# Head with x tiles 3 to 7 gated on half of v's weights, v's norms in batches, and pool weights times projection as one matrix formed on the chip

## The reference, cut to what matters

```python
h = rmsnorm(x, g_mix); proj = h @ w_in             # a | u,v | gate_a | gate_b
a = proj[..., :512]                                # pooling branch, 4 groups of 128 columns
z = gelu(proj[..., 512:1536])                      # u and v of the gating branch
gate_a, gate_b = sigmoid(proj[..., 1536:2560]), sigmoid(proj[..., 2560:])
# pooling: per group g, window w = 2, 4, 8, 16
p = window_sum(a_g, w) / min(w, pos+1) - a_g
pa = einsum('btgc,gcd->btgd', p, w_pool).reshape(B, T, 512) * s_pool
# gating: chunks of 128 rows, causal 128 x 128 matrix per group
v = rmsnorm(z[..., 512:], g_v)
sg = u * (tril(w_s) @ v + b_s)
merged = gate_a * (pa @ w_pool_out) + gate_b * (sg @ w_gmlp_out)
x = x + merged @ w_out
h2 = rmsnorm(x, g_ffn)
x = x + (silu(h2 @ w_gate) * (h2 @ w_up)) @ w_down  # d_ff 2816
y = rmsnorm(x, g_final)
```

## Time and profile before

| | us |
|---|---|
| median of 3 runs (lowest, highest) | 832.25 (831.86, 832.78) |
| profiled execution, its own time | 831.42 |
| span of its slowest core (core 2), first to last instruction | 829.6 |
| spans of the 8 cores | 826.4 to 829.6 |
| PE busy in the span | 805.8 (97%) |
| DVE, ACT, POOL busy | 380.8 (46%), 225.0 (27%), 96.2 (12%) |

### The profile page before, as it was taken

The page is one execution under the profiler, slowest core; times in us unless marked ns, Lnnn a source line. Parts: engine busy times, 40 slices in busy tenths (PEclk is TensorE's granted clock), DMA queues, the critical chain, the costliest instruction groups (busy, mean ns, idle before and its releaser), DMA issues.

```text
span 829.6 us, 12893 instructions; the slowest of 8 cores (826.4 to 829.6 us)
## 1 busy us (share of the span) xinstructions
PE 805.8 (97%) x4423; PEld 425.6 (51%) x4474; DVE 380.8 (46%) x618; ACT 225.0 (27%) x458; POOL 96.2 (12%) x154
## 2 busy tenths in 40 slices
PE   5999999999999999999999999999999999999996
PEld 3465666645666666644444444444444444444442
DVE  3776444468222222265776935446711111115357
ACT  2654322224211211120136352322321111110023
POOL 2720000012000000000312000011200000000001
PEclk9999999999999999999999999999999999999998
DMA  7894155684974543354977417688576444336313
GB/s 167 182 181 84 26 77 77 102 122 86 198 114 69 80 74 66 63 92 65 144 238 112 77 28 135 112 170 136 95 117 102 77 77 77 66 62 102 51 48 155
DMA packets 57315, 85.14 MB, mean 103 GB/s; under 512 B 23373, under 2 KB 23749, under 8 KB 57236
## 3 DMA queue, kind: packets, MB, share of 16 engines
q0 software_dynamic: 30352, 57.97, 45.3%
q1 hardware_dynamic: 26755, 26.09, 11.3%
q10 hardware_dynamic: 146, 0.27, 0.1%
HBM read 128.72 MB, written 9.01 MB: 166 GB/s over the span
## 4 chain that ended last, share of the span: by engine, by line
PE 84%; DVE 6%; issue 3%; DMA 2%; POOL 2%; ACT 2%; DVEq 0%; SPq 0%; POOLq 0%; ACTq 0%
PE ps L347 81%; DMA xbuf<-xp 2%; POOL rs L384 1%; DVE xbuf L367 1%; ACT junk L375 1%; ACT junk L992 1%; DVE xbuf L984 1%; PE ps L746 1%; PE ps L742 1%; DVE ybuf L1017 1%; DVE hb L404 0%; POOL rs L1003 0%; PE ps L695 0%; DVE shr L627 0%; DVE xbuf L874 0%
## 5 line engine op out<-in xcount | busy, mean ns | idle before, releaser
L347 PE MATMUL ps<-hT,ring 128*128 128x384 bf16 (+2 forms) x2698 | 484.1, 337 | 1.2
L347 PEld LDWEIGHTS ps<-hT,ring 128*128 128x128 bf16 x2720 | 265.5, 98 | 206.3
L347 PE MATMUL ps<-ring,ovl 128*128 128x512 bf16 x939 | 207.3, 379 | 1.1
L846 DVE TENSOR_TENSOR ovl<-ftmp,ps 128x384 bf16<-128x384 f32 (+2 forms) x110 | 64.2, 584 | 233.8 <-PE ps L347 226.5
L347 PEld LDWEIGHTS ps<-ring,ovl 128*128 128x128 bf16 x960 | 93.5, 98 | 113.8 <-issue 2.2
L844 ACT ACTIVATE ftmp<-ps 128x384 f32<-128x384 f32 (+2 forms) x110 | 56.3, 515 | 232.0 <-PE ps L347 232.0
L267 POOL DMA_DIRECT2D ring<-wpk x60 | 45.0, 750 | 493.8 <-PE ps L347 459.9
L944 DVE TENSOR_TENSOR xbuf<-xbuf,ps 128x512 f32<-128x512 f32 x64 | 43.4, 687 | 41.2 <-PE ps L347 41.1
L347 PE MATMUL ps<-ovl,ring 128*128 128x384 bf16 (+2 forms) x317 | 62.0, 337 | 0.2
L812 DVE TENSOR_TENSOR shr<-shr,ps 128x384 f32<-128x384 f32 (+2 forms) x40 | 23.4, 585 | 83.3 <-PE ps L347 74.5
L992 ACT ACTIVATE junk<-xbuf 128x512 bf16<-128x512 f32 (+1 forms) x34 | 21.3, 627 | 124.0 <-DVE xbuf L984 120.9
(11 more groups left out here) (90 smaller groups left out, 346.8 us busy)
## 6 DMA issues: line engine op xcount, KB each, us to landing
ring<-wpk POOLq DMA_DIRECT2D x48, 1024.0 KB, 11.2
xbuf<-xp SPq DMA_DIRECT2D x16, 512.0 KB, 6.6
yp<-ybuf SPq DMA_DIRECT2D x11, 512.0 KB, 3.4
ring<-wpk POOLq DMA_DIRECT2D x8, 512.0 KB, 13.0
ring<-wpk POOLq DMA_DIRECT2D x4, 768.0 KB, 8.1
yp<-shr SPq DMA_DIRECT2D x4, 512.0 KB, 2.6
AB<-xp SPq DMA_DIRECT2D x2, 512.0 KB, 6.9
shr<-xp SPq DMA_DIRECT2D x2, 512.0 KB, 11.6
```

What stands on the lines that cost most here:

```text
L347: ins = e.matmul(out=out, lhsT=lhs_fn(i), rhs=rhs_fn(i), start=(i == 0), stop=(i == n - 1))
L846: P.op('dve', lambda e: e.tensor_tensor(out=actT[:, f, c0:c0 + W], in0=ftmp[:, fi, :W], in1=PS[bU][:, :W], op=ALU.mult), reads=[('ftmp', f ...
```

## The change

- Loads: tiles 0, 1, 2 and the samples are issued at once. Ring block 0 is loaded in two halves (`ring_issue_halves`), both after tile 0 has landed; tiles 3 to 7 wait for the first half. Blocks 0 and 1 are read in pieces of 2048 and 4096 elements. Block 1 is issued at step 7, the constants at 8, block 2 at 9.
- v: a tile's eight matmuls may stand in two groups of four (`v_part`), and for the first tiles they do. gelu(v) goes to its own buffer per tile (`vg`, in the space of `mergedT`; samples in `ftmp`), the squares come some steps later, and POOL makes the means and rs of three tiles in one pair of operations (`v_rs`).
- The rows of g_v and two small vectors are copied on DVE at step 3 (`row_later`); the transpose of w_s moves from g = 0 to g = 2; the window sums of g = 2 are deferred too, but for their first three operations.
- `b4` is gone, and `paT`. ACT scales `w_pool`, which is handed over transposed, with `s_pool` (four operations of 128x128); for each q PE multiplies it with the quarter of `w_pool_out` (four matmuls of 256 columns), ACT copies the products to `mpo`, and the gates stage multiplies `mpo` with `pooled`. `mpo` is kept for `s` = 1, whose blocks hold `w_gmlp_out` alone. In the gates the product with `sgT` now stands ahead of the one with `pooled`.

```diff
-WPIECE = 1024
+WPIECE = [2048 if i < 1 else 4096 if i < 2 else 1024 for i in range(len(WBLOCKS))]
...
+        vg = ovl[:, 8 * TW + 9 * 512:8 * TW + 9 * 512 + 8 * 1024].bitcast(F32).rearrange("p (n c) -> p n c", n=8)
...
-        blocks = offs * NSUP
+        blocks = list(offs)
+        for (o_, e_), blk in zip(offs, WBLOCKS):
+            blocks.append((o_ + 128 * 1024, 1024) if blk[0][0] == 'w_po' else (o_, e_))
...
+        def ring_issue_halves(j, after=()):
+            slot = j % NSLOT
+            off, ne = blocks[j]
+            for h_ in range(2):
+                dst = ring[:, slot, h_ * (ne // 2):(h_ + 1) * (ne // 2)]
+                src = wpk[0:1, off + h_ * 64 * ne:off + (h_ + 1) * 64 * ne].rearrange("o (p e) -> (o p) e", p=128)
+                P.dma('pool',
+                      (lambda e, dst=dst, src=src: e.dma_start(out=dst, in_=src)),
+                      'wh%d' % h_, reads=list(after), writes=[('ring', slot, h_)])
             rstate['issued'] = j + 1
...
-        for slot in range(2, 8):
-            xload(0, slot, after=[('x', 1, 0)])
+        xload(0, 2)
         cdma('pool', ident_b[:, :], c_ident[:, :], 'ident_b', own='c_idb')
-        ring_issue(0)
+        ring_issue_halves(0, after=[('x', 0, 0)])
+        for slot in range(3, 8):
+            xload(0, slot, after=[('ring', 0, 0)])
...
-            ring_issue(1)
             cdma('pool', ws_nat[:, :, :], w_s.rearrange("g i j -> i g j"), 'ws_nat', own='c_wsnat')
-            cdma('pool', wpool_b[:, :, :], w_pool.rearrange("g c d -> c g d"), 'wpool', own='c_wpool')
             cdma('pool', bs_row[:, :], b_s[0:1, :], 'bs_row', own='c_bsrow')
...
+            cd(ybuf[:, 2, 0:512], w_pool[:, :], ('ybuf', 2))
...
+                    def fn(e, wv=wv):
+                        ins = None
+                        for i in range(4 * h_, 4 * h_ + 4):
+                            ins = e.matmul(out=PS[b][:R, :], lhsT=hT[:, i, col0:col0 + R], rhs=wv[:, i, :],
+                                           start=(i == 0), stop=(i == 7))
+                        return ins
+                    P.op('pe', fn, reads=[cres_[h_]] + hT_res([slot]), writes=[('ps', b)])
+
+                def v_mm(t_):
+                    if t_ == 0:
+                        v_part(0, 0)
+                    elif t_ == 1:
+                        v_part(1, 0)
+                        v_part(0, 1)
+                    elif t_ == 2:
+                        v_part(1, 1)
+                        v_part(2, 0)
+                        v_part(2, 1)
+                    else:
+                        v_part(t_, 0)
+                        v_part(t_, 1)
...
+                def v_rs(lo, hi):
+                    ka, kb = kv[lo], kv[hi - 1] + 1
+                    P.op('pool', lambda e: e.tensor_scalar(out=ms[:, ka:kb], in0=ss[:, ka:kb], scalar1=1.0 / 512,
+                                                           scalar2=EPS, op0=ALU.mult, op1=ALU.add),
+                         reads=[('ss', k_) for k_ in range(ka, kb)], writes=[('ms', k_) for k_ in range(ka, kb)])
+                    P.op('pool', lambda e: e.tensor_tensor(out=rs[:, ka:kb], in0=ms[:, ka:kb],
+                                                           in1=mhalf[:, 0:1].to_broadcast([128, kb - ka]), op=ALU.pow),
+                         reads=[('ms', k_) for k_ in range(ka, kb)] + ['mhalf'],
+                         writes=[('rs', k_) for k_ in range(ka, kb)])
...
+                vsq_at = {9: (0, 1), 10: (2, 3), 11: (4, 5), 12: (6,), 13: (7,), 14: (8,)}
+                vrs_at = {11: 0, 12: 3, 14: 6}
-                for i_ in range(n_ + 8):
-                    at(i_ - 3, do_v)
+                for i_ in range(n_ + 6):
+                    at(i_ - 4, v_mm)
...
+                    if i_ == 3:
+                        while row_later:
+                            row_later.pop(0)()
...
-                    at(i_ - 6, lambda t_: vst[t_][0]())
-                    at(i_ - 6, lambda t_: vst[t_][1]())
-                    if i_ == 5:
+                    at(i_ - 5, v_gelu)
+                    for t_ in vsq_at.get(i_, ()):
+                        v_sq(t_)
+                    if i_ == 7:
+                        ring_issue(1)
+                    if i_ == 8:
                         late_pool_consts()
                         mid_sp_consts()
-                    if i_ == 8:
+                    if i_ == 9:
                         ring_issue(2)
+                    if i_ in vrs_at:
+                        lo_ = vrs_at[i_]
+                        v_rs(lo_, lo_ + 3)
+                        for t_ in range(lo_, lo_ + 3):
+                            v_out(t_)
...
-                if s == 0 and g == 0:
+                if s == 0 and g == 2:
...
-                pool_chain(defer=(g == 3))
+                if g == 3:
+                    for _ in range(3):
+                        deferred_ops.pop(0)()
+                pool_chain(defer=(g >= 2))
...
-                    for (c0, W, tl) in nts:
-                        b = bank()
-                        pres = [('pooled', g)] + ([('pooled', g, 's')] if c0 + W > TPS else [])
-                        P.op('pe', lambda e, b=b, g=g, c0=c0, W=W: e.matmul(
-                            out=PS[b][:, :W], lhsT=wpool_b[:, g, :], rhs=pooled[:, g, c0:c0 + W],
-                            start=True, stop=True),
-                             reads=pres + ['wpool'], writes=[('ps', b)])
-                        P.op('act', lambda e, b=b, g=g, c0=c0, W=W: e.activation(
-                            out=paT[:, g, c0:c0 + W], in_=PS[b][:, :W], func=AF.Copy, scale=spT[:, g:g + 1]),
-                             reads=['spT'], writes=[('paT', g, c0), ('ps', b)])
...
-                if g < 3:
-                    b4_list[g]()
+            if s == 0:
+                for g_ in range(4):
+                    P.op('act', lambda e, g_=g_: e.activation(out=wpool_b[:, g_, :],
+                                                              in_=ybuf[:, 2, g_ * 128:(g_ + 1) * 128],
+                                                              func=AF.Copy, scale=spT[:, g_:g_ + 1]),
+                         reads=[('ybuf', 2), 'spT'], writes=[('wpool', g_)])
             while deferred_ops:
...
+                        if s == 0 and dl == 0 and c0 == 0:
+                            for h_ in range(2):
+                                bM = bank()
+
+                                def mpo_mm(e, bM=bM, h_=h_, pow_=pow_):
+                                    ins = None
+                                    for j_ in range(2):
+                                        ins = e.matmul(out=PS[bM][:, j_ * 256:(j_ + 1) * 256],
+                                                       lhsT=wpool_b[:, 2 * h_ + j_, :], rhs=pow_[:, 2 * h_ + j_, :],
+                                                       start=True, stop=True)
+                                    return ins
+                                P.op('pe', mpo_mm, reads=fres + [('wpool', 2 * h_), ('wpool', 2 * h_ + 1)],
+                                     writes=[('ps', bM)])
+                                P.op('act', lambda e, bM=bM, h_=h_, q=q: e.activation(
+                                    out=mpo[:, 2 * h_:2 * h_ + 2, q * 256:(q + 1) * 256],
+                                    in_=PS[bM][:, :].rearrange("p (j c) -> p j c", j=2), func=AF.Copy),
+                                     writes=[('mpo', q, h_), ('ps', bM)])
...
-                        P.op('pe', mm_group(PS[bP][:, :W],
-                                            lambda i, dl=dl, pow_=pow_: pow_[:, i, dl * 128:(dl + 1) * 128],
-                                            lambda i, c0=c0, W=W: paT[:, i, c0:c0 + W], 4),
-                             reads=fres + [('paT', gg, c0) for gg in range(4)], writes=[('ps', bP)])
...
+                        P.op('pe', mm_group(PS[bP][:, :W],
+                                            lambda i, d=d: mpo[:, i, d * 128:(d + 1) * 128],
+                                            lambda i, c0=c0, W=W: pooled[:, i, c0:c0 + W], 4),
+                             reads=[('mpo', q, h_) for h_ in range(2)] + [('pooled', gg) for gg in range(4)]
+                             + ([('pooled', gg, 's') for gg in range(4)] if c0 + W > TPS else []), writes=[('ps', bP)])
...
```

108 lines of the change are left out of this document (73 added, 35 removed).

## The result

The changed kernel took 835.17 us (833.76 to 836.52, 5 runs) against 832.25 (831.08 to 832.78, 5 runs) before: a ratio of 1.0043, 95% interval 1.0031 to 1.0054. By the ratio it is slower by some 3.6 us (by the medians alone 2.9), where 824.0 was forecast and 821 to 828.5 was the range. The times in this document are medians of all executions of a kernel, also of those in which the cores of a die ran at a lower granted clock; the ratios leave those out. The profiled execution took 835.17, its slowest core 833.6. Where before all cores lay within a few us, there are now two groups, of 824 to 827 and of 832 to 834.

A forecast was written before the change was run, and what follows sets the result against it. It took PE's own work and the start of stage 2 (a), which sets the end one for one, as the bound. From 831.4: -4.7 - 1.4 - 3.56 + 1.75 + 0.1 = -7.8, so 823.6, given as 824.0; range 821 to 828.5.

The forecast's parts named there:

- issue near 25, as before: Head, POOL's queue: ring block 1, behind the eighth norm, is issued near 25 and lands at 35, before stage a at 37.3.
- 15 us are enough: SP's constants: `w_pool`, the last, is not read before 52, and 15 us suffice for its landing.
- rival 3: Start of a: ring block 1, issued late, lands at 47.7 and a waits for it; 834.0 us, chance 0.05.
- Block 2 ... costs nothing: Ring block 2, for u: it has 14 us more than block 1, so its later issue costs 0.
- The clock behind a wait: Behind PE's wait in u: a lowered clock cost core 3 0.8 us; its removal is only in part 2's bound of -2.2.
- The head, -4.7: Stretch up to stage 2 (a): a's start on the slowest core moves from 42.0 to 37.3; bounds -7 and 0.
- The rate of 0.15 MB in one us: Head's loads: the ring's queue alone moves 0.15 MB per us, so half of v's weights (0.52 MB) costs 3.5 us.
- the first half would have the engines for itself: Head's loads: block 0's first half uses the engines from 8.3, lands near 12; the second shares with x 3 to 7.
- rival 1: Head: DMA engines are the bound, or PE stays at 1.2 GHz; a starts at 40, 826.3 us, chance 0.21.
- Part 2, -1.4: Waits in u: PE's 1.40 us wait for DVE's window sums goes; bounds 0 and -2.2.
- Part 3: `b4` removed: -3.56 us on PE; added 16 matmuls +1.75 and the gates' wait for `mpo` +0.1.
- The batch of v's norms: Head: 18 POOL operations become 6, off PE's path; window sums start 5.3 us behind a's start, not 8.7.

The follow-up runs named there:

- e2: Changed kernel with ring block 1 issued at step 5 of the head's loop, not step 7: 828.30 us, ratio 0.9967 to the kernel before.
- e9: e3 with ring block 1, the constants and ring block 2 at steps 7, 8, 9, not 5, 5, 8: 837.87 us, ratio 1.0076 to the kernel before.
- e1: Changed kernel with SP's constants waiting for x tile 7, not ring block 1: 836.52 us, ratio 1.0044 to the kernel before.
- e17: e6 with 20 more matmuls without a reader ahead of tile 3's transposes: 826.84 us, ratio 0.9944 to the kernel before.
- e5: Changed kernel with x tiles 3 to 7 waiting for x1, not the first half of block 0: 835.60 us, ratio 1.0042 to the kernel before.
- e16: e6 without loading block 0's second half (1 MB less), as many matmuls: 824.37 us, ratio 0.9909 to the kernel before.
- e3: Changed kernel with every hunk of the head taken back, the rest kept: 828.51 us, ratio 0.9955 to the kernel before.
- e6: Changed kernel with the edits of e5 and e2 together: 827.71 us, ratio 0.9962 to the kernel before.
- e13: e6 with ring block 1 in pieces of 1024 elements, not 4096: 828.61 us, ratio 0.9959 to the kernel before.
- e14: e6 with 48 more matmuls without a reader, 16 ahead of v and 32 behind tile 4's transposes: 830.38 us, ratio 0.9978 to the kernel before.
- e4: Changed kernel with SP's constants waiting for ring block 2, not block 1: 844.35 us, ratio 1.0147 to the kernel before.

## Why the prediction was wrong, step by step

- **"issue near 25, as before"** is the step that turned the sign: the cost of moving block 1 by two steps was put at nothing. I put ring block 1 behind the eighth norm and worked out 25 from gelu and squares that all came 3 to 4 us later. It was issued at 29.2 in the mean. Moved back by two steps it goes at 23.8 and the kernel is faster than before (e2); the old head loses as well when block 1 and what stands behind it move later by as much (e9).
- **"15 us are enough"** for SP's constants looked at `w_pool` alone. All of them, `sel` and `ident_f` with their readers in u ahead of `w_pool`'s, hang on block 1's landing; they took 16.5 and 18.7 on core 1. My rival 3 had the right place (block 1's landing) and the wrong victim: it asked only when a itself would wait for the ring, and gave 834.0 with a chance of 0.05. In the changed kernel no core waited for the ring ahead of a or in u; they waited for what was gated on it. And "Block 2 ... costs nothing" held only while the constants were the later ones (e1).
- **The clock behind a wait**, which I charged with 0.8 on one core as the earlier trace rows, cost 2.2 on core 1. The Trainium skill, TensorE: Matmul & The Clock Gate, "What's actually happening", says that the low clock is the default and sustained work lifts it. This trace agrees: granted 0.50 from 62 to 68 on core 1, while cores 0 and 4, which did not wait, have 1.00. That each such wait costs the clock is not so: e1's core 4 waited 2.90 in u and kept 1.00.
- **The head, -4.7**, did not come: a's latest start is 42.5 for 42.0, its mean 41.1 for 40.0, which two single profiles can't tell from no change. Of core 1's miss of 11.8 it is 3.7. Two terms, from the forecast's 36.7 to 41.1: tile 3's transposes at 23.8, not 20.5, and from there to a 17.3, not 16.2. The second is the clock: at full clock it is 15.4 (e17), less than I had. The first is the transfers. The first half took 8.4 us from issue to landing (7.26 to 15.63 on core 1) and not about 6, so tile 3 was issued at 15.7 and not 12. The rate of 0.15 MB in one us was right. From 11 to 13 the ring's queue filled the engines of core 1 alone and moved 0.32 MB:

```profile
q0 software_dynamic: 79, 0.32, 101.0%
```

  What was wrong is that the first half would have the engines for itself: by 15.6 that queue had moved 0.9 MB, nearly both halves (1.05 MB). Taking tile 3's gate off did not bring it sooner (e5), a megabyte less to read did (e16). That e16's a is at 36.7, the forecast's value, is chance: its terms are 21.3 and 15.4, the forecast's 20.5 and 16.2. Starting v 2.6 us sooner is right (15.2 for 17.8), and buys nothing, since v's early tiles then wait for tile 3. That is rival 1, with its 0.21, and its 40 for a was 1 too early.
- **Part 2, -1.4**, right: no wait for DVE in u on the cores that had their constants. **Part 3** right within 0.6: the wait ahead of the first product with `mpo` is 0.7 on six cores and 0.9 on two, not 0.1. Their sum is shown by e3: 785.1 to 785.4 for 784.5.
- **Core by core** the sum: forecast 37.3 + 784.5 = 821.8. Core 1 has 41.0 + 792.6: 3.7 from the head, 5.5 from two waits, 2.2 from the clock, 0.4 from the rest.
- **The sum itself**: 823.6 + 0.8 is 824.4, not 824.0, and 0.58 + 0.21 + 0.10 is 0.89, not 0.90. Neither matters beside a miss of 11 us.
- **The batch of v's norms, the pieces of block 1, DMA block 2**: nothing to be seen either way (e2 and e6 keep the batch and are level with e3; e13).

## What to carry over

Before a transfer is moved by a step or two, draw the DMA engines' busy share over the stretch and list everything that is gated on its landing, not only its own reader: here an idle stretch of 5 us ahead of a full one of 28 was paid at its end by whoever came last, and taking the gate off that one only handed the bill on (e1). An earlier start of one engine is worth nothing if the next input comes when it did before; and matmuls without a reader, put into the gap that stays, cost what they take wherever PE is not idle (e14), while what they bring where it is idle lies within the noise here (e17 against e6).

## What the runs showed of the hardware

Transfers on SP's queue of 60 and 64 KB, which landed in 4.1 and 11.4 us where they were issued near 30 (e1, core 1), took 16.5 and 18.7 when issued at 43.5 and 45.0 into a stretch whose DMA share was 1.02, with ring block 2 in flight and blocks 3 and 4 issued from 44.7 on (core 1 of the changed kernel); 1 MB of ring issued at 33.9 took 27.0 us there, 12.9 in the kernel before and 10.5 for the block issued into the idle engines. Waits of PE in u were followed by a granted clock of 0.50 for some us on the cores where they came to 2.9 to 5.5 in the changed kernel (1, 2, 5 and 7), but a single one of 2.9 on e1's core 4 was not (1.00 there from 56 to 68). In the head, PE was busy for 5.9 of the 10 us from 14 to 24 on core 5 of the changed kernel and had 0.50 from 18 to 30; with 20 matmuls without a reader in the gap it had 1.00 from 20 on (e17); five other cores had that in e6 without them.

The DMA share alone does not tell when a small transfer lands. On cores 0 and 3 of the changed kernel the share from 32 to 60 was 1.04 and `ident_f` landed in 10.9 and 9.7:

```profile
ident_f<-c_ident SPq DMA_DIRECT2D x1, 64.0 KB, 10.9
```

What goes with the landing time is how long ahead of ring block 3 `ident_f` was issued. Over the eight cores of the fourteen kernels that gate it on block 1 (all of the table but e1 and e4) it took 14.4 to 20.3 where it was issued less than 1.8 us ahead of block 3, or behind it, 9.7 to 16.7 from 1.9 to 2.7 ahead, and 6.5 to 15.3 from 2.8 on. Block 1 at step 5 brought this lead (4.8 to 8.5 in e2, -0.3 to 3.3 in the changed kernel). The relation is read from the traces; no run moved the one without the other.

The Trainium skill, DMA: Bandwidth & Descriptors, "Queues, rings and completion order", says that each DMA engine takes its queues in turn, packet by packet. That SP's small transfers are slowed and not stopped beside ring blocks fits it; how much of their 16 to 19 us is the ring's packets and how much what stands ahead of them on SP's own queue (`stb`, 480 KB) no run here separates.
